# A decoder layer with routed experts: residual rows in another order, no token turns before the experts, and one more weight slot

## The reference

```python
x = x + mixing_block(rmsnorm(x, norm_mix), ...)       # w_in 2048x5120, RG-LRU and short conv, w_out 2048x2048
x = x + cross_attention(rmsnorm(x, norm_xattn), ...)  # w_q, w_k, w_v, w_o, 256 memory tokens, caches
x = x + hier_moe(rmsnorm(x, norm_moe), ...)
y = rmsnorm(x, norm_final)

def hier_moe(h, wg, bg, we, be, w_gate, w_up, w_down):
    g_sel = argmax(softmax(h @ wg + bg))              # 1 of 4 groups
    top_p, top_i = top_k(softmax((h @ we + be)[group g_sel]), 2)   # 2 of its 4 experts
    gate = one_hot(...) * wts                         # 16 experts, two of them not zero for a token
    act = silu(h @ w_gate[e]) * (h @ w_up[e]) * gate  # w_gate, w_up: 2048x512 for each expert
    return sum_e act @ w_down[e]                      # w_down: 512x2048
```

## Time and profile before

| | |
|---|---|
| median of 3 runs | 1483.22 us (1483.09 to 1483.44) |
| profiled execution | 1484.51 us |
| its span, first to last instruction | 1482.8 us |
| TensorE busy | 1427.7 us |
| first expert starts | 999.24 us |
| last down tile's matmuls start | 1454.20 us |

### The profile page before, as it was taken

The page is one execution under the profiler, slowest core; times in us unless marked ns, Lnnn a source line. Parts: engine busy times, 40 slices in busy tenths (PEclk is TensorE's granted clock), DMA queues, the critical chain, the costliest instruction groups (busy, mean ns, idle before and its releaser), DMA issues.

```text
span 1482.8 us, 25563 instructions
## 1 busy us (share of the span) xinstructions
PE 1427.7 (96%) x9308; PEld 1089.8 (73%) x9308; DVE 555.9 (37%) x1067; ACT 190.1 (13%) x392; POOL 796.8 (54%) x1453
## 2 busy tenths in 40 slices
PE   6999999999999999999999999979999999999997
PEld 6999999998889999998777799963334334344344
DVE  3546578829575342222111342151112122122123
ACT  5100321000000010003222200051000000000003
POOL 3777587979987757763444467512451440522500
PEclk8999999999999999999999999989999999999999
DMA  8344344445654444464788744747999999999993
GB/s 256 124 161 142 107 150 129 155 145 176 208 167 162 142 166 143 146 236 191 299 318 310 248 152 154 293 189 323 421 421 422 422 422 422 422 422 422 422 422 140
DMA packets 106120, 377.07 MB, mean 254 GB/s; under 512 B 12421, under 2 KB 12421, under 8 KB 76290
## 3 DMA queue, kind: packets, MB, share of 16 engines
q1 hardware_dynamic: 103778, 371.68, 65.8%
q10 hardware_dynamic: 2272, 4.42, 0.9%
HBM read 369.30 MB, written 6.77 MB: 254 GB/s over the span
## 4 chain that ended last, share of the span: by engine, by line
PE 83%; DMA 10%; DVE 3%; ACT 2%; issue 1%; SPq 1%; POOL 0%; POOLq 0%; ACTq 0%; DVEq 0%
PE ps L840 40%; PE ps L897 13%; PE ps L1184 11%; DMA tiles<-in_expert_w_up 8%; PE ps L1250 4%; PE ps L1214 3%; PE ps L966 2%; DMA tiles<-in_expert_w_down 2%; PE ps L790 1%; PE ps L1201 1%; PE ps L984 1%; PE ps L974 1%; PE ps L1005 1%; DMA A<-in_norm_final 1%; PE ps L1032 0%
## 5 line engine op out<-in xcount | busy, mean ns | idle before, releaser
L749 POOL COPY A<-A 128x16 f32 x952 | 146.1, 213 | 289.4 <-issue 289.3
L840 PE MATMUL ps<-hT,tiles 128*128 128x144 f32 x1792 | 295.3, 288 | 3.4 <-ACT A L1406 1.5
L840 PE MATMUL ps<-A,tiles 128*128 128x144 f32 x1792 | 262.0, 286 | 0.8 <-DVE A L2003 0.7
L840 PEld LDWEIGHTS ps<-hT,tiles 128*128 128x128 f32 x1792 | 251.6, 191 | 5.0 <-issue 2.6
L840 PEld LDWEIGHTS ps<-A,tiles 128*128 128x128 f32 x1792 | 237.0, 190 | 1.9 <-DVE A L2003 0.9
L702 POOL TENSOR_TENSOR tiles<-tiles 128x512 f32<-128x512 f32 x88 | 117.3, 1333 | 173.4 <-DMA tiles<-in_w_in 70.4
L840 PE MATMUL ps<-tiles 128*128 128x144 f32 x960 | 171.1, 287 | 0.0
L1184 PE MATMUL ps<-tiles,A 128*64 128x512 f32 x512 | 147.0, 601 | 13.2 <-DMA A<-in_expert_w_up 6.4
L840 PEld LDWEIGHTS ps<-tiles 128*128 128x128 f32 x960 | 140.4, 191 | 0.0
L897 PE MATMUL ps<-tiles,mT 128*128 128x256 f32 x512 | 132.9, 382 | 1.0 <-ACT kv_stage L1440 1.0
L1709 DVE COPY pair_sums<-ps 128x144 f32<-128x144 f32 x44 | 13.5, 308 | 300.4 <-PE ps L840 300.4
(11 more groups left out here) (350 smaller groups left out, 1698.6 us busy)
## 6 DMA issues: line engine op xcount, KB each, us to landing
tiles<-in_expert_w_down SPq DMA_DIRECT2D x56, 1024.0 KB, 22.4
tiles<-in_w_in SPq DMA_DIRECT2D x40, 1024.0 KB, 5.1
tiles<-in_expert_w_gate SPq DMA_DIRECT2D x32, 1024.0 KB, 22.1
tiles<-in_expert_w_up SPq DMA_DIRECT2D x32, 1024.0 KB, 22.5
A<-in_expert_w_up SPq DMA_DIRECT2D x24, 1024.0 KB, 25.2
tiles<-in_xa_w_k SPq DMA_DIRECT2D x16, 1024.0 KB, 5.1
tiles<-in_w_out SPq DMA_DIRECT2D x16, 1024.0 KB, 5.1
tiles<-in_xa_w_q SPq DMA_DIRECT2D x16, 1024.0 KB, 5.1
```

The costliest lines, as they stand in the source:

```text
L749: m = nc.gpsimd.tensor_copy(xe[:, :, at + n:at + n + 1], h_moe_or_zero[:, :, bass.ds(token, 1)])
L840: return mm(one(u + mp, x, TH), w[:, kp, mp, :], rhs, start=(first and g == 0 and kp == 0), stop=(g == 3 and kp == 1), skip_group_check=True)
```

## The change

Block b = 4g + k of the residual now holds feature 512g + 4n + k at partition n (`fourths`). This is the order in which expert tiles are now read, `"e (g p k) f -> e g p k f"`, and w_in, w_q and the router weights too (`turned_tiles_of`); w_out and w_o keep their loads, and their columns are split with a step of four instead. The gain rows for the residual (8 rows) are transposed a second time in that order, and the output is put back into order when the result is read from PSUM. The token turns, `h_moe`, `h_tok` and the column of zeros are gone: gathers read `hT` directly, empty slots read token 0. The root goes into the expert instead: `take_roots` (six matmuls) picks the root of each slot, ScalarE copies it (`roots_out`) and uses it as the scale of the SiLU; for the up branch it is multiplied into the gates. The router logits get a unit of their own. In the order of PSUM events, places, pick_0, root_0 and counts follow each other. `MOE_SLOTS` is 15: slots 12 and 13 lie where the attention's result was, slot 14 in the memory tokens' buffer `mT`; all three are loaded once w_o is done. Slots 3 to 11 are used twice in 24 tiles, the others once.

```diff
-PE_EVENTS, MOE_SLOTS = 11, 14
+PE_EVENTS, MOE_SLOTS, REUSE = 11, 15, 12
...
+        def fourths(x, b):
+            return x.rearrange("p (g n k) -> p g k n", k=KT, n=P)[:, b // KT, b % KT, :]
...
-        def quarter_blocks(t):
-            w = tile_of(t).rearrange("p (kp kk) (mp mm n) -> p kk mm kp mp n", kk=2, mp=2, mm=2)
+        def quarter_blocks(name, t):
+            w = tile_of(t)
+            if name in ("w_out", "w_o"):
+                w = w.rearrange("p (kp kk) (n mp mm) -> p kk mm kp mp n", kk=2, mp=2, mm=2)
+            else:
+                w = w.rearrange("p (kp kk) (mp mm n) -> p kk mm kp mp n", kk=2, mp=2, mm=2)
...
         def moe_slot(m):
-            m %= 24
-            return m if m in (12, 13) else m % 12
+            return m % 24 if m % 24 < MOE_SLOTS else m % 24 - REUSE
+        def moe_uses(m):
+            return 2 if MOE_SLOTS <= moe_slot(m) + REUSE < 24 else 1
         def moe_lag(m):
-            return 24 if m % 12 < 2 else 12
+            return REUSE if m % 24 >= MOE_SLOTS else 24 - REUSE if moe_uses(m) == 2 else 24
...
+        def turned_tiles_of(w):
+            return w.rearrange("(g p k) m -> g p k m", k=KT, p=P)
+        w_in, w_q = (turned_tiles_of(a[n][0]) for n in ("w_in", "xa_w_q"))
+        w_route = [turned_tiles_of(a[n][0]) for n in ("router_group_w", "router_expert_w")]
-        e_gate = a["expert_w_gate"][0].rearrange("e (p g k) f -> e g p k f", k=KT, p=P)
+        e_gate = a["expert_w_gate"][0].rearrange("e (g p k) f -> e g p k f", k=KT, p=P)
...                                   # SP: router weights, 8 loads instead of 2
+            for g in range(KT):
+                sp.dma_start(wr[:, KT * g:KT * g + KT, 0:NG], w_route[0][g]).then_inc(wr_loaded, 16)
+                sp.dma_start(wr[:, KT * g:KT * g + KT, NG:NG + NE], w_route[1][g]).then_inc(wr_loaded, 16)
...
                 elif m >= 12:
-                    after_event(sp, EVENT["h_tok_rest"] + 1)
+                    sp.wait_ge(tile_used, TILE["moe"])
...                                   # TensorE, at the start
+                m = nc.tensor.transpose(bank(u, b // 4)[:, at + NROWS:at + NROWS + TURNED], fourths(pack[0:TURNED, :], b),
+                                        ident[0:TURNED, 0:TURNED])
...                                   # TensorE, after the place sums
+            def take_roots(out):
+                for s in range(2):
+                    for c in range(3):
+                        n = own_rows[c]
+                        m = mm(out[:, s:s + 1], pick[0:n, c, C * s:C * s + C], h_rstd[0:n, c:c + 1], start=(c == 0), stop=(c == 2))
+                return m
+            pe.wait_ge(tokens_numbered, 1)
+            pe.wait_ge(pick_ready, 1)
+            number_slots(first_slot_sums)
+            take_roots(first_slot_roots).then_inc(unit_done, 1)
             for k in range(3):       # the counts
...                                   # TensorE, second branch of each pass
                 pe.wait_ge(pick_ready, plus(n // 2 + 1, i, 1))
+                take_roots(slot_roots)
                 number_slots(slot_sums)
...                                   # TensorE, ahead of the first expert
-            read_out(pe, UNIT["h_moe_rest"])
             read_out(pe, UNIT["places"])
-            pe.wait_ge(h_moe_out, 3)
             pe.wait_ge(xe_ready, 1)
...                                   # ScalarE
-                fn(silu[0:C, :], ps[0:C, 4 + s, :], ACT.Silu).then_inc(silu_ready, 1)
+                fn(silu[0:C, :], ps[0:C, 4 + s, :], ACT.Silu, scale=slot_root[0:C, s:s + 1]).then_inc(silu_ready, 1)
...                                   # ScalarE, behind its 56 gathered slots
+            after_event(act, EVENT["root_0"])
+            roots_out(first_slot_roots)
+            u = UNIT["places"]
+            act.wait_ge(slot_root_out, 1)
+            act.sem_inc(half_free[u % 2], 1)
...                                   # VectorE
-            v.tensor_copy(tab[:, 0, :], bank(u, 3)[:, 0:NE]).then_inc(half_free[u % 2], 2)
+            v.tensor_copy(tab[:, 0, :], bank(u, 3)[:, 0:NE]).then_inc(half_free[u % 2], 1)
...
+            then(tt(G(11), G(11), h_rstd[:, 0:3].unsqueeze(2).broadcast_to([P, 3, 4]), ALU.mult))
```

More of the change, by code:

```diff
@@ L64 @@
 NX = NJ - NE
+WARM = 0
 TILE, _t = {}, 0
@@ L75 @@
                ("w_k", 3), ("mix_stat", 1), ("states", 1), ("w_k_last", 1), ("w_out", 8), ("w_q", 8),
-               ("values", 8), ("heads", 2), ("w_o", 8), ("router", 1), ("h_tok", 3), ("h_moe", 1),
-               ("places", 1), ("h_moe_rest", 1), ("final_stat", 1), ("y", 3)):
+               ("values", 8), ("heads", 2), ("w_o", 8), ("router", 1), ("logits", 1),
+               ("places", 1), ("final_stat", 1), ("y", 3)):
     UNIT[_n] = _u
@@ L251, in build @@
         token_no, at = cut(at, 4)
+        actT, at = cut(at, 2, KT, C)
         assert at <= 17088
@@ L472, in tokens_of_slots @@
             _, tokens = nc.values_load_multi_w_load_instructions(
-                slot_row(p, first, n), engines=[engine], min_val=0, max_val=T,
-                skip_runtime_bounds_check_because="a slot's sum over the tokens holds at most one token's number, 1 to T")
+                slot_row(p, first, n), engines=[engine], min_val=0, max_val=T - 1,
+                skip_runtime_bounds_check_because="a slot's sum over the tokens holds at most one token's number, 0 to T - 1")
             return tokens
@@ L1142, in _ @@
             m.then_inc(unit_done, 1)
-            for c in range(1, 3):
-                start_unit(pe, UNIT["h_tok"] + c)
-                turn_tokens(c, range(DB)).then_inc(unit_done, 1)
-            def turn_back_chunk(c, unit):
-                start_unit(pe, unit)
-                turn_back(c, lambda b: bank(unit, b // 4)[:, b % 4 * P:(b % 4 + 1) * P])
-            turn_back_chunk(0, UNIT["h_moe"])
             u = UNIT["places"]
@@ L1161, in _ @@
             m.then_inc(unit_done, 1)
-            for k in range(3):
-                n = own_rows[k]
-                m = mm(bank(u, 3)[:, 0:NE], ones[0:n, :], mask16[0:n, k, :], start=(k == 0), stop=(k == 2))
-            m.then_inc(unit_done, 1)
             def number_slots(out):
@@ L1172, in number_slots @@
                 m.then_inc(unit_done, 1)
+            def take_roots(out):
[8 more added lines that the diff above has]
+            take_roots(first_slot_roots).then_inc(unit_done, 1)
+            for k in range(3):
+                n = own_rows[k]
+                m = mm(bank(u, 3)[:, 0:NE], ones[0:n, :], mask16[0:n, k, :], start=(k == 0), stop=(k == 2))
+            m.then_inc(unit_done, 1)
             BRANCH_BANK, PLACE_BANK, ACT_BANK = 4, 6, 7
@@ L1255, in down @@
                         m.then_inc(tile_used, 2)
[L1257 to L1262 removed]
+            for n in range(WARM):
+                wait_moe_tile(pe, n // KT)
+                mm(ps[:, ACT_BANK, :], ident[:, :], moe_tile(n // KT)[:, n % KT * TW:(n % KT + 1) * TW], start=True, stop=True)
             read_out(pe, UNIT["places"])
[L1264 removed]
             pe.wait_ge(xe_ready, 1)
@@ L1545, in slots_numbered, with roots_out @@
                 copy(slot_row(p, 0, 2 * C), sums).then_inc(slots_out, 1)
-            act.wait_ge(token_rstd_ready, 1)
-            for c in range(3):
-                tokens_out(c)
-            after_event(act, EVENT["h_moe"])
-            turned_back(0, UNIT["h_moe"])
+            def roots_out(roots):
+                copy(slot_root[0:C, :], roots).then_inc(slot_root_out, 1)
             act.wait_ge(gate_in, 2)
```

175 lines of the change are left out of this document (74 added, 101 removed).

## The result

The kernel after takes 1610.07 us (median of 4 runs, 1607.46 to 1611.71), the kernel before beside it 1483.33 us: ratio 1.0848, interval 1.0829 to 1.0867. It is 127 us slower; the forecast was 1483.8 and no change. The profiled execution took 1607.46 us with a span of 1605.7, against 1482.8 before: 122.9 more to explain.

A forecast was written before the change was run, and what follows sets the result against it. Bound: TensorE almost without gaps to 968.71 us, then the weight stream's restart after the router, tiles left and tail. Terms +1.2 + 0 + 0.8 - 1.55 + 0.1 = +0.55 us took 1483.22 to 1483.8; range 1479 to 1510.

The forecast's parts named there:

- The strides: w_out and w_o tiles read with a 16-byte step by TensorE and GpSimd: 0 taken for both, called the largest unknown.
- The other end: TensorE's w_out and w_o weight loads: the alternative to no price, a doubled load time for strided reads.
- rival 2: Strided weight loads outlast their matmuls by 0.1 us, 32 records x 32 tiles: +100 us, 1580; chance 0.16.
- The start: Kernel start, before the projections: eight more gain-row transposes add +1.2 us (0 to 3); other operand views keep their counts.
- The eight more transposes: TensorE's turned gain rows at the start: 0.15 us each, as the existing eight take 1.21 us, so +1.2 us.
- The router stage: Between w_o and first expert: removed turns gain nothing, ScalarE's and VectorE's queues eat 5 us; start 999.2 against 999.24: 0.
- Slots known: Router stage, end of ScalarE's cast after slot numbering: at 988.6, 5 us before h_moe is complete in the kernel before.
- Clock and slot: Expert loop's start: longer lower clock delays four tiles by +0.8 us; tile 14 loaded beforehand gives -1.55 us.
- The forecast of 0.8: First four expert tiles at 1.2 GHz: 0 if the low clock lasts as now, 1.7 us if twice; +0.8 taken.
- the cover: Expert loop: root sums' 1 to 1.8 us a pass hide behind the stream's 59.65; +0.1 at the end, 7 x 1.5 uncovered.
- the 7.1 from which TensorE would wait: GpSimd's four sums a tile in w_o: TensorE waits above 7.1 us; forecast lay between 5.1 and 8.9, below 7.1.
- My 0: GpSimd's strided sums in w_out and w_o: taken to stay below TensorE's waiting point, so no added time.

The follow-up runs named there:

- adj_both: The kernel after, but TensorE and GpSimd both read the w_out and w_o tiles in adjacent quarters again: 1496.30 us, ratio to before 1.0082.
- before_strided: The kernel before, but both engines read w_out and w_o with the step of 16 bytes: 1595.91 us, ratio to before 1.0756.
- adj_all: The kernel after with all TensorE's strided stationary operands (w_out, w_o, x, gains, scatter rows) and GpSimd's reads made adjacent: 1485.65 us, ratio to before 1.0009.
- early: The kernel after, but ScalarE copies roots before its gathered slots and TensorE makes counts before slot numbers and roots: 1607.23 us, ratio to before 1.0819.
- adj_tensor: The kernel after, but TensorE alone reads w_out and w_o adjacent, waiting earlier for GpSimd's still strided sums: 1510.68 us, ratio to before 1.0179.
- natural: Against the kernel after: residual rows in natural order, all reads adjacent, expert gate and up rows in 2 KB packets: 1506.36 us, ratio to before 1.0155.
- pair: The kernel after's plan with pairs instead of fourths: reads step two elements, gate and up rows in 4 KB packets: 1497.88 us, ratio to before 1.0094.
- step2: The kernel after, but TensorE and GpSimd read w_out and w_o with a step of two elements (8 bytes): 1497.32 us, ratio to before 1.0084.

## Why the prediction was wrong

**The step that failed** is "The strides", in the price of TensorE's weight loads: "That is the nearest row for a weight load; I take 0, with a doubled load as the other end." The other end came true. Its rival 2 sized it with 0.1 us on 32 records of 32 tiles, +100 us; adj_both and before_strided measured 113.8 and 112.1. So the mechanism and its price were on the page, and only the choice between the two ends was wrong; rival 2 had a chance of 0.16, and the range ended at 1510, below it. Two reasons:

- The nearest row was the wrong kind of row. ScalarE's 216 ns for 16 elements, against 213 for 12, look like a small instruction's fixed time, and reading 16 elements could hide a doubled rate inside it. A weight load reads 128 elements of each partition behind a matmul that leaves no slack (0.19 us of load, a record every 0.12). The stride has to be priced on rows whose time is their reading.
- The memset (127 against 125 ns for half as many elements) pointed the other way and I used it for GpSimd only, though it may be a fixed time as well. The Trainium skill's rule of two hits in a line ("SBUF — State Buffer", cachelines), cited and set aside for ScalarE's row, agrees with every step tried.

Rival 2's price was partly luck. By its own figures a doubled load is 2 x 0.13 = 0.26 us, 0.14 above the matmul's 0.12 and not 0.1: 143 us for 1024 records. And 1483 + 100 is 1583, not 1580. The measured 0.11 a record lies by the rounded value.

**The start** was taken at +1.2 us and is +13.7 (33.67 to 47.40), of which 2.7 are swallowed before 120 us. I wrote that "the other operand views at the start keep their counts" and gave the strided x no price, so rival 2 lacked it too. It is 9.6 us for 96 scaled turns (22.73 to 13.11 in adj_all, where part of them ran at a granted clock of 0.50). The eight more transposes were mis-sized as well. The timeline of after, the first four of 16 and the last:

```profile
14.73 0.38 PE L820 MATMUL ps<-ident,A 71*128 71x71 f32 x1 [5.24 <-DMA A<-in_norm_final]
15.04 0.29 PE L821 MATMUL ps<-ident,A 8*128 8x8 f32 x1
15.26 0.38 PE L820 MATMUL ps<-ident,A 71*128 71x71 f32 x1
15.57 0.29 PE L821 MATMUL ps<-ident,A 8*128 8x8 f32 x1
...
18.73 0.28 PE L821 MATMUL ps<-ident,A 8*128 8x8 f32 x1
```

Eight of one shape took 1.21 us. Sixteen that alternate between 71 and 8 rows take 4.3 (14.73 to 19.0): 0.31 and 0.22 us apart instead of 0.15. That each change of shape is what costs is argued, not shown: with the strided read of the gains gone (adj_all) the same 16 still take 4.2 us, but no run has eight and then eight. The term is +3 us instead of +1.2.

**The router stage** was right in sum and in what gates it, with errors of single terms that partly cancel. Forecast: the first expert 30.5 us after w_o as before, measured 30.48. Slots known at +19.9, measured +20.3 (1112.57). The place sums took 2.84 us from 1106.01, where I took 1.9; the root sums 1.69 where I took 2.8; the counts 1.57 where I took 1.4. From there over ScalarE's 56 slots to TensorE's start: 10.05 + 0.5 forecast, 10.18 measured (1112.57 to 1122.75). VectorE's part ended at 1121.40 and GpSimd's 24 slots at 1117.77, so ScalarE was last. So ScalarE's queue ate the gain, as early shows; VectorE's ended 1.1 us sooner than ScalarE's root copy began.

**Clock and slot.** SP's queue in after:

```profile
1132.31 0.35 SPq L639 DMA_DIRECT2D A<-in_expert_w_up  x1
1135.73 0.35 SPq L639 DMA_DIRECT2D kv_stage<-in_expert_w_down  x1
```

The first load of the loop comes 9.56 us after the first expert, 8.79 before: +0.77, forecast +0.8. The granted clock is 0.50 (1.2 GHz) until about 1127.4 in after, 4.6 us into the expert, and until 1002.3 in before, 3.1 us into it; at half pace the 1.5 us more cost 0.75. In adj_all they are 6.0 us, and the load comes 10.24 after: +1.45. The forecast of 0.8 was a value chosen between 0 and 1.7, so its closeness in after is partly luck. Tile 15 stands alone and tile 16 follows 3.42 us later, forecast 3.4. From that first load to the last tile used it is 444.68 us against 446.17: -1.49, forecast -1.55 with +0.1 for the root sums. A TensorE-bound pass takes 57.6 us (1158.99 to 1216.61 in the down tiles' starts), 1.9 more than the 55.75 of before, hidden behind the stream's 59.65 as forecast. The root sums are only about 0.8 of it: adj_all, whose scatter reads adjacent, takes 56.6 (1095.43 to 1152.01), and the other 1.0 is the scatter's strided loads, which the prediction left out. In after's last pass the cover is used up: the last two down stretches follow on each other without a DMA between.

**GpSimd.** The four sums in w_out take 6.37 us a tile in after and 5.22 in adj_both, between my 5.1 and 8.9 and under the 7.1 from which TensorE would wait. In after TensorE's own slowness hides them in any case, so the 0 is not tested there: with TensorE fast and GpSimd strided, adj_tensor lost 14.4 us, an upper end, since its wait stands earlier. My 0 was too low for that case. By the Trainium skill, "GPSIMD Engine Reference", section "Performance pitfalls for Q7 kernels", the estimate was 7.8; the trace has less. What I had not seen is that these sums hold up VectorE, whose own sums were the last that TensorE waited for.

## What to carry to other kernels

Price a stride on the engine whose time is its reading, above all TensorE's weight loads, which have no slack behind a short matmul (0.11 us a record behind 144 columns, 0.03 behind 288); where no row has it, and the two ends are 100 us apart, the first thing to measure is that row, and the range has to hold both ends. A permutation of features has three bills, and each wants its own row: the step within a partition (free up to 8 bytes here), the packet from memory (2.49, 2.56 and 2.71 us a MB for 8, 4 and 2 KB) and the queues behind which freed work now stands. A removed stage gives nothing until the signal of every engine ahead of the next one is issued earlier, too.

## What the runs showed of the hardware

- In w_o, behind 144 columns, a weight load of 128 x 128 fp32 with a step of 16 bytes lets a record out every 0.234 us, with 32 bytes every 0.238, with 4 or 8 bytes every 0.123. The granted clock is 1.00 in all of them.
- The strided loads set their own pace whatever clock is granted: the 96 scaled turns take 22.73 us in after, where the clock is 1.00 up to 35 us, and 22.73 in adj_both, where it is 0.50 for their first 4 us. Adjacent, they take 11.93 us at 1.00 (natural) and 13.11 where the clock is 0.50 for the first 4 us (adj_all).
- For transposes the runs give no such comparison at one clock: 32 of x take 5.65 us with a step of 16 bytes (after, mean granted clock 0.68), 4.87 with 8 bytes (pair, 0.61) and 3.08 adjacent (adj_all, 1.00).
- A VectorE instruction that meets a sum of GpSimd takes about as long as that sum: 0.50 us alone, 1.52 beside an adjacent one, up to 2.37 beside a strided one.
- GpSimd's four sums of a tile take 5.22 us adjacent, 5.26 with a step of 8 bytes (step2) and 6.37 with 16.
- Transposes that alternate between two row counts stand 0.27 us apart on the mean, where eight of one shape stand 0.15 apart.
